# A ring of four weight slabs split in place, its transfers released by TensorE

## The reference

```python
# first block, layer by layer
h = h + mixer(rms_norm(h))               # layer 0: chunk gating; layer 1: dilated attention (qkv 1024 -> 4608)
h = h + square(relu(y @ w_up)) @ w_down  # y = rms_norm(h); 1024 -> 4096 -> 1024
...
# second block; shift, scale, gate come from silu(c) @ ada_w + ada_b, 1024 -> 9216 for each layer
h = modulate(rms_norm(x), shift, scale)
x = x + 0.5 * gate * swiglu(h, ffn_w_in, ffn_w_out)   # 1024 -> 2 x 2816 -> 1024, twice a layer
x = x + gate * mixer(h)                  # layer 0: pooling; layer 1: gated convolution, between the two
```

## Time and profile before

| what | value |
|---|---|
| median of 3 runs (range) | 1641.51 us (1639.99 to 1641.93) |
| span of the profiled execution, first to last instruction | 1638.8 us |
| the profiled execution's own time | not listed apart from its span; the median of the runs stands 2.7 us above the span |
| PE busy | 1559.3 us (95%) |
| DVE busy | 1052.6 us (64%) |
| ACT busy | 708.3 us (43%) |
| moved by DMA | 345.84 MB, mean 211 GB/s |
| mean granted TensorE clock | 0.959 |

### The profile page before, as it was taken

One profiled execution on the slowest core, in us unless ns is written; L12 is line 12 of the kernel. 1 busy time (PEld: TensorE's weight loads), 2 busy tenths in 40 slices (PEclk: granted clock), 3 DMA queues, 4 the chain that ended last, 5 costly groups with the idle time before them and its releaser, 6 DMA issues.

```text
span 1638.8 us, 20523 instructions
## 1 busy us (share of the span) xinstructions
PE 1559.3 (95%) x7069; PEld 1284.2 (78%) x7069; DVE 1052.6 (64%) x1126; ACT 708.3 (43%) x831; POOL 22.1 (1%) x63
## 2 busy tenths in 40 slices
PE   6899999999999999989999799999999999999997
PEld 4778888788787888768888688887788878778886
DVE  4758677546535867667888678887655465665444
ACT  5345444444324454453444344435343454354342
POOL 1000000000000000000000000000000000000000
PEclk9999999999559999989999899999999999999999
DMA  8438877457303788847899258996555546445552
GB/s 259 173 138 306 293 268 253 158 176 262 105 20 136 275 283 286 287 151 234 308 311 322 81 192 301 311 322 220 165 194 179 187 128 224 144 150 194 180 185 85
DMA packets 201893, 345.84 MB, mean 211 GB/s; under 512 B 9531, under 2 KB 105027, under 8 KB 201836
## 3 DMA queue, kind: packets, MB, share of 16 engines
q1 hardware_dynamic: 161420, 267.22, 48.6%
q10 hardware_dynamic: 40416, 77.86, 13.5%
HBM read 343.96 MB, written 1.09 MB: 211 GB/s over the span
## 4 chain that ended last, share of the span: by engine, by line
PE 84%; DVE 8%; ACT 3%; issue 2%; DMA 2%; POOL 1%; SPq 0%; POOLq 0%; DVEq 0%; ACTq 0%
PE up_ps L1320 50%; PE acc L1320 29%; DVE w_lo L867 3%; PE tr_ps L1401 2%; DMA ada_raw<-in_ada_w 1%; PE tr_ps L1320 1%; DVE ada_acc L935 1%; PE tr_ps L1586 1%; ACT w_hi L514 1%; ACT xn L536 1%; ACT xn L551 1%; DVE res L973 1%; DVE xn L970 1%; POOL rstd L472 1%; PE tr_ps L1500 1%
## 5 line engine op out<-in xcount | busy, mean ns | idle before, releaser
L867 DVE TENSOR_TENSOR w_lo<-raw,w_hi 128x2048 fp32r<-128x2048 f32 x245 | 561.1, 2291 | 303.1 <-ACT w_hi L514 301.8
L514 ACT ACTIVATE w_hi<-raw 128x2048 fp32r<-128x2048 f32 x245 | 469.5, 1916 | 313.3 <-PE up_ps L1320 255.5
L1320 PE MATMUL up_ps<-w_hi,xT_hi 128*128 128x512 f32 x1264 | 505.2, 400 | 22.2 <-DVE xT_lo L889 17.0
L1320 PE MATMUL up_ps<-w_hi,xT_lo 128*128 128x512 f32 x1264 | 497.3, 393 | 0.0
L1320 PE MATMUL up_ps<-w_lo,xT_hi 128*128 128x512 f32 x1264 | 496.8, 393 | 0.0
L1320 PEld LDWEIGHTS up_ps<-w_hi,xT_hi 128*128 128x128 f32 x1264 | 240.3, 190 | 74.9 <-issue 17.6
L1320 PEld LDWEIGHTS up_ps<-w_hi,xT_lo 128*128 128x128 f32 x1264 | 240.0, 190 | 51.4
L1320 PEld LDWEIGHTS up_ps<-w_lo,xT_hi 128*128 128x128 f32 x1264 | 240.5, 190 | 47.8
L935 DVE SCALAR_TENSOR_TENSOR ada_acc<-ada_raw,cond,ada_acc 128x512 f32 (+1 forms) x252 | 189.3, 751 | 15.7 <-DMA ada_raw<-in_ada_w 8.0
L1320 PE MATMUL acc<-w_hi,hT_hi 128*128 128x512 f32 x624 | 193.4, 391 | 4.1 <-DVE hT_lo L878 4.1
L1320 PE MATMUL acc<-w_hi,hT_lo 128*128 128x512 f32 x624 | 192.4, 389 | 0.0
(11 more groups left out here) (121 smaller groups left out, 855.2 us busy)
## 6 DMA issues: line engine op xcount, KB each, us to landing
raw<-in_ffn_w_in SPq DMA_DIRECT2D x176, 512.0 KB, 4.8
ada_raw<-in_ada_w ACTq DMA_DIRECT2D x72, 1024.0 KB, 7.1
raw<-in_ffn_w_out SPq DMA_DIRECT2D x88, 512.0 KB, 4.4
raw<-in_w_up SPq DMA_DIRECT2D x64, 512.0 KB, 4.6
raw<-in_w_down SPq DMA_DIRECT2D x64, 512.0 KB, 4.8
raw<-in_b_w_qkv SPq DMA_DIRECT2D x36, 512.0 KB, 4.5
raw<-in_conv_w_in SPq DMA_DIRECT2D x24, 512.0 KB, 4.7
raw<-in_a_w_in SPq DMA_DIRECT2D x16, 512.0 KB, 6.3
```

The costliest lines, as they stand in the source:

```text
L514: nc.scalar.activation(w_hi[:, slot, :], raw[:, slot, :], ACT.Copy).then_inc(hi_ready, 1)
L867: nc.vector.tensor_tensor(w_lo[:, slot, :], raw[:, slot, :], w_hi[:, slot, :].bitcast(F32), ALU.subtract).then_inc(lo_ready, 1)
L1320: return nc.tensor.matmul(dst, a, b, start=start, stop=stop, skip_group_check=True)
```

## The change

- `w_lo` has no memory of its own: it is laid over `raw`, and the subtraction writes where it reads. Raw, `w_lo` and `w_hi` are rings of four slots (eight slabs of memory instead of nine).
- A transfer of slab n waits for `slab_used` of slab n-4, no longer for the split of slab n-3. The splits wait for landing (ScalarE) and for the high part (VectorE), no longer for `slab_used`.
- `ahead(g)` still splits slab g+3 (`LEAD = 3`).
- The loops follow from the ring of four: MLP loop one step to a body (six rounds), FFN loop four steps to a body (two rounds), qkv without a loop on SP, ACT and DVE. Thresholds of waits are scaled to fit.

```diff
-RING = 3
+RING = 4
+LEAD = 3
-MLP_BODY = 3
+MLP_BODY = 1
+FFN_BODY = 4
...
+        raw_at = -(-nc.sbuf_base // 32) * 32
         raw = sb("raw", [P, RING, SLAB])
+        w_lo = nc.alloc_sbuf_tensor_at("w_lo", [P, RING, SLAB], F32R, offset=raw_at)
         w_hi = sb("w_hi", [P, RING, SLAB], F32R)
-        w_lo = sb("w_lo", [P, RING, SLAB], F32R)
...
                     if n >= RING:
-                        sp.wait_ge(hi_ready, n - RING + 1)
-                        sp.wait_ge(lo_ready, n - RING + 1)
+                        sp.wait_ge(slab_used, n - RING + 1)
...
                     act.wait_ge(raw_landed[slot], 32 * (n // RING + 1))
-                    if n >= RING:
-                        act.wait_ge(slab_used, n - RING + 1)
...
                     dve.wait_ge(hi_ready, n + 1)
-                    if n >= RING:
-                        dve.wait_ge(slab_used, n - RING + 1)
...
             def ahead(g, i=None, per=0):
-                n = g + RING
+                n = g + LEAD
...
-                with pe.Fori(0, FFN_CHUNKS - 3) as i:
-                    step(2, False, i)
+                with pe.Fori(0, FFN_BODIES) as i:
+                    for b in range(FFN_BODY):
+                        step(2 + b, False, i)
```

More of the change, by code:

```diff
@@ L385, in _ @@
             g0 = at["qkv"].slab
[L386 to L389, removed]
+            for c in range(9):
+                for s in range(2):
+                    load(g0 + 2 * c + s, up_src(b_w_qkv[0], s, c * UPN), up_view)
             sp.wait_ge(bias_stored, 16)
@@ L422, in ffn @@
                 load(g0 + 4, down_src(w_out, 0), down_view)
[L423 to L426, removed]
+                with sp.Fori(0, FFN_BODIES) as i:
+                    for b in range(FFN_BODY):
+                        for s in range(2):
+                            load((g0 + 5 + 3 * b + s, i * (3 * FFN_BODY)),
+                                 ffn_src(w_in, s, (i * FFN_BODY + (b + 2)) * HALF), ffn_view)
+                        load((g0 + 7 + 3 * b, i * (3 * FFN_BODY)), down_src(w_out, (i * FFN_BODY + (b + 1)) * HALF),
+                             down_view)
+                g1 = g0 + 3 * FFN_CHUNKS - 4
+                for s in range(2):
+                    load(g1 + s, ffn_src(w_in, s, (FFN_CHUNKS - 1) * HALF), ffn_view)
+                load(g1 + 2, down_src(w_out, (FFN_CHUNKS - 2) * HALF), down_view)
                 load(g0 + 3 * FFN_CHUNKS - 1, down_src(w_out, (FFN_CHUNKS - 1) * HALF), down_view)
@@ L674, in _ @@
             stage = [mid, pre, xn]
[L675 to L685, removed]
+            for c in range(6):
+                g = p.slab + 2 * c
+                ahead(g)
+                for t in range(TT):
+                    if t == 0:
+                        act.wait_ge(up0_ready, p.up + c + 1)
+                    else:
+                        act.wait_ge(slab_used, g + 2)
+                    nc.scalar.activation(stage[c % 3][:, t, 0:UPN], up_ps[:, t, :], ACT.Copy).then_inc(qkv_copied, 1)
+                ahead(g + 1)
             for b in range(3):
@@ L773, in step @@
                     transposed(c, i)
-                    ahead(g + 2, i, 3)
+                    ahead(g + 2, i, 3 * FFN_BODY)
                 g = p.slab
@@ L782, in ffn @@
                 step(1, g + 2)
-                with act.Fori(0, FFN_CHUNKS - 3) as i:
-                    step(2, g + 5, i)
+                with act.Fori(0, FFN_BODIES) as i:
+                    for b in range(FFN_BODY):
+                        step(2 + b, g + 5 + 3 * b, i)
                 begin(FFN_CHUNKS - 1, g + 3 * FFN_CHUNKS - 4)
@@ L1078, in _ @@
             tr0 = p.tr + NORM_FILLS
[L1079 to L1090, removed]
+            for b in range(6):
+                g = p.slab + 2 * b
+                ahead(g)
+                for c in ((), (0,), (1, 2), (), (3,), (4, 5))[b]:
+                    for t in range(TT):
+                        tr = tr0 + TT * c + t
+                        dve.wait_ge(tr_ready, tr + 1)
+                        nc.vector.tensor_copy(qkT[:, 4 * c:4 * c + 4, t * P:(t + 1) * P],
+                                              tr_ps[:, tr % 2, :].rearrange("p (f n) -> p f n", n=P))\
+                            .then_inc(tr_read, 1)
+                ahead(g + 1)
             for b in range(3):
@@ L1183, in begin @@
                             modulation(name, m)
[L1184 removed]
+                    ahead(g, i, 3 * FFN_BODY)
                     if unit0 is not None and c >= 2:
[L1186 removed]
+                        ada(unit0 + c - 2, 0, i, FFN_BODY)
                     gated_mid(c, i)
[L1188 removed]
+                    ahead(g + 1, i, 3 * FFN_BODY)
                     if c == 1:
@@ L1213, in ffn @@
                 step(1, g + 2)
-                with dve.Fori(0, FFN_CHUNKS - 3) as i:
-                    step(2, g + 5, i)
+                with dve.Fori(0, FFN_BODIES) as i:
+                    for b in range(FFN_BODY):
+                        step(2 + b, g + 5 + 3 * b, i)
                 begin(FFN_CHUNKS - 1, g + 3 * FFN_CHUNKS - 4)
@@ L1650, in step @@
                             modulation(name, m, 0)
-                    down_slab(gb + 2, hT_hi, hT_lo, 0, start, i, 3, (mid_fill(p, name, c - 1), 1, 2))
+                    down_slab(gb + 2, hT_hi, hT_lo, 0, start, i, 3 * FFN_BODY,
+                              (mid_fill(p, name, c - 1), 1, 2 * FFN_BODY))
                     if start:
```

35 lines of the change are left out of this document (17 added, 18 removed).

## The result

The changed kernel takes 1654.24 us, median of four executions (1647.96 to 1656.38), the kernel before 1640.75 us beside it (1639.24 to 1641.93). The ratio is 1.0075, 95% interval [1.0055, 1.0095]: slower, by 12 us by the ratio (13.5 us between the medians).

What follows compares the result with a forecast made beforehand. The prediction took TensorE to bound the kernel inside the loops; saved waits of -1.35, -0.70 and -0.40 us sum to -2.45 us, taking 1641.51 to 1639.1 us, in a range from 1635.5 to 1648 us.

Steps and rivals of the forecast that it cites:

- Depth in a loop: Loads in the loops, now issued when TensorE finishes a slab: landing may take 8.3 us, so cost 0.
- Rival A: FFN steps of ffn0 and ffn1: slabs land late beside ada and delay `mid`, +13 to +31 us; chance 12%.
- Entry of attention: Second slab of `attn_out`, issued later, lands at 407.1 without delaying attention: 0, bounds -0.6 and +2.5 us.
- Start: Ahead of the first GELU: ScalarE splits slab 3 earlier and PE's stall goes, -1.35 us, bounds -1.35 and 0.
- End of mlp1: PE's wait for `hT_lo` after the turn shrinks as the ada transfer lands first: -0.70 us, bounds -0.70 and +2.
- Step 1 of mlp1: PE's 1.08 us wait for VectorE shrinks as the split stops waiting for `slab_used`: -0.40 us, bounds -1.08 and 0.
- Splits in place and loop bodies: Subtractions over their own operand, and longer FFN and shorter MLP loop bodies: each taken to cost 0.
- rival B: Long back edges in four FFN stages each cost a late instruction fetch: +4 to +8 us, 1646 us; chance 5%.

Runs made afterwards that it cites:

- both: Changed kernel with hT_hi and hT_lo made before the second split ahead in each FFN's last step, and attention's entry reordered: 1640.60 us, ratio 0.9983.
- gelu: Kernel before, with ScalarE in gate_in's first chunk applying GELU to the first tile before splitting the fourth slab: 1639.79 us, ratio 0.9984.
- unrolled_only: Kernel before with SyncE's load loops written out and nothing else: 1642.28 us, ratio 1.0000.
- loops: Kernel before with the FFN loops written four steps to a body, three slabs and all waits as they were: 1641.25 us, ratio 0.9994.
- ffn_tail: Changed kernel with hT_hi and hT_lo made before the second split ahead in the last step of all four FFNs: 1645.92 us, ratio 1.0014.
- tail_ffn0: Changed kernel with hT_hi and hT_lo made before the second split ahead in the last step of ffn0 alone: 1650.39 us, ratio 1.0044.

## Why the prediction was wrong

Predicted were 1639.1 us, in a range to 1648.0, with 0.20 on slower; measured are 1654.24 and 1657.01.

- *The step that failed is "Depth in a loop".* It worked out the slack of a landing, 8.3 us, for the full step of ffn1 and put the cost "in the loops with ada" and in stages without it at 0. That holds in both profiles of the changed kernel: the loop's steps take 16.79 to 16.82 us. But the sum had no term for the last, shortened step behind each loop. There the split stands ahead of `hT_hi` and `hT_lo`, and TensorE needs these at once. The landing there took 8.4 us and made the wait 3.1 us longer (3.57 - 0.48); in ffn0 it was 2.3 us (2.75 - 0.47). I read the loop's body and costed its period. ffn1's second step, ahead of the loop, had no term either and cost 1.2 us.
- *Rival A* had the mechanism, a load that waits for TensorE and shares the engines with ada, and 9 us as the landing that would hurt. It had the wrong place, `mid` in each of 18 steps, where neither profile of the changed kernel waits; its chance of 12% was set by the rows of a steady step. Its event does exist: a landing of 10.4 us gave a wait of 1.74 us, near the 1.7 us that it forecast for 10 us, but in one step of one profile (both).
- *Entry of attention*: taken as 0 with a bound of +2.5, measured 2.9 and 2.9 us. The slab of `attn_out` came as I had it: its split starts at 404.57, or at 407.06 with the lead of 2.49 us added back, and I had it landed at 407.1. I followed this slab alone and missed the ada transfer that is now issued beside it: it took 12.3 us to land in place of 5.3, and everything on VectorE, the logits too, stood behind it.
- *Start*: -1.35 us was right as a stall, which is gone. But it needs neither a fourth slot nor the split in place (gelu).
- *End of mlp1*: -0.70 didn't come. PE waits 1.62 and 1.26 us there in the two profiles, against 1.67; in unrolled_only, loops and gelu, which keep the old release, it is 1.87, 1.18 and 1.48, so the row that I started from varies by itself.
- *Step 1 of mlp1*: -0.40 was mis-sized: 0.96 and 1.10 us of wait against 1.08, near 0.
- *Splits in place and loop bodies*: 0, right: 2290 ns, and 0.9994 for the FFN bodies alone, with four long back edges, against what rival B supposed.
- *The price of a stall*: I took a wait's length as its cost. Behind a stall of 3.57 us the clock was 0.66 for 5 us, and ffn1 lost 4.7 us at its end with 3.1 us more of wait.

## What to carry to other kernels

When a buffer's release moves later, don't ask only whether the consumer gets its data in time. Ask of each queue what stands behind the first instruction that will now wait, and ask it at the ends of loops and the seams between stages, where a step is shorter than its period: there most of the 12 us were lost by an order that was harmless while the data was always early. Put work that the bottleneck needs now ahead of splits for later. And before adding a buffer against a stall, try whether an order does it: the one stall that this change removed, 1.35 us at the start, goes as well when one line is moved.

## What was not expected of the hardware

- The same program's time depends on where the clock drops. The changed kernel's two profiles are 0.5 us apart at 43 us (TensorE's transposes start at 42.66 and 43.16) and 4.3 us at mlp0. The stretch behind these transposes, first and second profile:

```profile
46.00:52.00 6.00, 6.00 (x29) 4.66 (x27) 5.24 (x8) 1.92 (x1) 0.03 (x1) 1.00 0.15 57
```
```profile
46.00:52.00 6.00, 6.00 (x18) 3.95 (x16) 4.38 (x5) 1.92 (x1) 0.00 (x0) 0.55 0.21 83
```

  TensorE is busy for all of the 6 us, at 0.55. In gelu's profile it is 0.50 too, in that of the kernel before 1.00. So the lead of 2.5 us with which the changed kernel reached qkv in its first profile was in good part this: of the five other kernels in the table none has it. Of the nine profiles in which the stall at 33 us is gone, eight have 0.50 to 0.63 in this stretch; of the four in which it stands, two have 1.00 and two 0.72. Whether taking the stall away brings the lower clock on is not shown. Single executions of one kernel spread by up to 12 us (gelu 1636.2 to 1642.9, ffn_tail 1639.3 to 1648.5, tail_ffn0 1642.8 to 1655.1), and nine to twelve of them still leave an interval 3 to 5 us wide, so a gain of 2 us is at the edge of what these runs can tell.
- An ada transfer of 1 MB is waited for until 12.3 us after its issue at attention's entry, where slabs of attn_out and mlp1 and the bias rows are issued beside it, against 7.1 us as the median of all 72. Of the slab at the end of ffn1 the slower half lands in 4.9 us when the ada transfer beside it is cut to 8 columns and in 8.4 us when it isn't; in single steps elsewhere such a half took 10.4 and 11.5 us.
